# Raw token rows with a root column, and a tenth weight slot requested at the start of the expert stage

## The chip, the cores and the metric

One core of one Trainium2 chip. The metric is the device time of one launch in microseconds (us). TensorE (PE in the profile), VectorE (DVE), ScalarE (ACT), GpSimd (POOL) and SyncE (SP) run their own instruction queues and meet only at semaphores. SP's queue issues nearly all transfers between memory (HBM) and the on-chip SBUF.

## What is computed

One inference step of a two-layer decoder over 288 tokens (256 prompt tokens, 32 sample tokens), all in float32. Each layer is a mixer (gated delta rule, then differential attention) followed by a mixture of experts. The change touches only the experts, cut here to what matters:

```
xn = x * rsqrt(mean(x*x) + 1e-6) * norm_m            # per token, 1024 columns
group = argmax(softmax(xn @ w_rg + b_rg))            # 1 of 4
e1, e2 = top 2 of the 8 experts of that group; gates from a softmax
hid = silu(xn @ w_gate[e]) * (xn @ w_up[e])          # 1024 -> 512
y   = hid @ w_down[e]                                # 512 -> 1024
out = gate1 * y[e1] + gate2 * y[e2];   x = x + out
```

There are 32 experts with three matrices of 2 MB each, so each layer streams about 201 MB of expert weights.

## The kernel before

`moe_phase` runs once per layer. It walks 16 main groups of two experts, 64 token places for each expert. TensorE turns the group's 128 gathered rows (`rows_T`), multiplies them with the gate and the up matrices (`stage`, L2540), turns the hidden rows (`hid_T`), multiplies with the down matrices (`products`, L2567), and adds the result of the group before to the tokens with selection matrices (`combine`, L2583).

**Weights.** Ten slots of 2 MB in SBUF form a ring; matrix p of the stream goes to slot p mod 10, and a group uses six. Slots 0 to 8 are prefetched in the mixer phase in front (in layer 1, slots 4 and 5 at the start of the expert phase). The space of slot 9, the tenth, holds `xn`, the normalized token rows, while the phase begins. So SP stores `xn` to memory (L2078), waits for the stores and for the semaphore `gx_T` of the first picks, and only then requests slot 9 (L2083, printed as L2838, the line of the helper `prefetch`). From then on SP requests a slot when TensorE has used up its old contents: `load(10)` (L2095) in halves after the first and the second half of the first gate product, then `load_whole` (L2104) pairs of 2 MB after the first up product, the first down product, and so on. All waits and requests on SP are in order.

**Start of the phase.** TensorE transposes the tokens, makes the router logits, fills its wait with 26 products of constants (`keep_busy`, L2503), and ranks the tokens by expert (L2508 to L2513). VectorE works out the choice of experts and writes `sel0`, six 128x64 selection tiles of 0 and 1 (L2309). With these TensorE picks the first group's rows straight from `xn` in SBUF (L2626, "the first picks"), makes a table of places (L2633) and begins the first gate product. ACT meanwhile squares the rows (L2188), takes the root (L2190) and normalizes them into `xn` (L2194). POOL clears the unused rows of `xn` (L2150, L2152) and the gather buffer `xg` (L2155). `xg`, `xgT` and others lie in `xrT`, `hid` lies in `norm_row` (router inputs), and `place_o` lies in `y_sb`.

**Later groups.** POOL gathers the rows of group n from memory (L2168) after `rows_T(n-1)`; ACT applies SiLU (L2210), and VectorE multiplies it with the up product (L2382); `hid_T` waits for that.

Of the kernel before, what the change touches and what calls it, by code (L numbers as in the profile page):

```python
# [8 lines left out]
F32 = mybir.dt.float32  # L9
# [1926 lines left out]
def moe_phase(nc, m, layer):  # L1936

    ctx, sems = ExitStack(), []
    with ctx:
# [6 lines left out]
        def sem(name):  # L1946
# [9 lines left out]
        sb("late_slots", [128, SLOT_COUNT - 7, SLOT_COLS])  # L1956
        xn = sb("last_slot", [128, SLOT_COLS])[:, 0:NT * D_MODEL].rearrange("p (t d) -> p t d", t=NT)
# [51 lines left out]
        sel0 = y_sb[:, 0:NT * 128].rearrange("p (t r) -> p t r", t=NT)  # L2009
        low = y_sb[:, NT * 128:NT * 128 + SLOTS]  # L2010
        BELOW = -1024.0
        xr_flat = xrT[:].rearrange("p k r -> p (k r)")
        xg = xr_flat[:, 0:1024]
        xgT = xr_flat[:, 1024:2048].rearrange("p (k r) -> p k r", k=KT)
        obf = xr_flat[0:1, 2048:2048 + 2 * OVER_GROUPS * N_EXPERTS].rearrange("p (b e) -> p b e", e=N_EXPERTS)
        selT = w_router.rearrange("p k n -> p (k n)")[:, 0:T_ALL]
        hid = norm_b[:, 0:512]
# [23 lines left out]
            "squares ss_cleared tail_cleared roots inverse normed xn_stored xT_made xT_kept folded logits_made logits_kept gdiff gexped tdiff texped hots ranked "  # L2041
# [6 lines left out]
        def by_tile(x):  # L2048
            return x.rearrange("p (k c) -> p k c", k=KT)
# [6 lines left out]
        xn_dram = m["xn_dram"]  # L2056
# [88 lines left out]
        def _(pool):  # L2145
# [4 lines left out]
            P.memset(xn[32:64, 2, :], 0.0).then_inc(s["tail_cleared"], 1)  # L2150
            pool.wait_ge(s["tail_cleared"], 1)
            P.memset(xn[64:128, 2, :], 0.0).then_inc(s["tail_cleared"], 1)  # L2152
            pool.wait_ge(s["tail_cleared"], 2)
# [3 lines left out]
            pool.wait_ge(s["xn_stored"], 16 * NT)  # L2157
            pool.wait_ge(s["table_ready"], 1)

            def gather(n, row):  # L2160

                if not isinstance(n, int) or n > 1:
                    pool.wait_ge(s["gathered"], n * 16 - 16)
# [743 lines left out]
```

## Time and profile before

| what | value |
|---|---|
| median of 3 runs | 1517.54 us (1515.52 to 1518.78) |
| the profiled execution: time, span | 1519.84 us, 1518.0 us |
| PE busy | 1469.2 us (97%) |
| DVE, ACT, POOL busy | 634.7, 284.9, 73.0 us |
| HBM read | 483.77 MB |
| GB/s in the steady part of both expert stages | 426 to 432 |
| granted TensorE clock, mean | 0.991 |

The page divides the span into 40 slices. In slices 11 to 21 and 30 to 39 both PE and the 16 DMA engines stand at 9 of 10: these are the two expert stages. PE's busy time is modelled, so "busy" does not say by itself that PE is what limits the stage; its idle times do.

### The profile page before, as it was taken

The page shows a single profiled execution, that of the slowest core. Times are in us where ns is not written, and L with a number is a line of the kernel's source. Part 1 is how long each engine was busy: PE and PEld are TensorE (multiplying, and loading weights), DVE is VectorE, ACT ScalarE, POOL GpSimd, SP SyncE. Part 2 cuts the span into 40 slices and gives each one's busy share as a digit, 9 for nine tenths or more (in the row PEclk, how much of TensorE's full clock was granted, in tenths as well). Part 3 has the DMA queues.
Part 4 walks back from the last instruction along what each step waited for, and adds up shares of the span by engine and source line. Part 5 has one row for each costly group of instructions (what it writes and reads, how often), then busy time and mean ns, then how long its engine had stood idle before and what let it go on. Part 6 is the DMA issues. An engine that isn't in the chain of part 4 may idle for free. (4 is left out here: it accounts for less than half of the span.)

```text
span 1518.0 us, 20246 instructions
## 1 busy us (share of the span) xinstructions
PE 1469.2 (97%) x7687; PEld 735.5 (48%) x7687; DVE 634.7 (42%) x1657; ACT 284.9 (19%) x746; POOL 73.0 (5%) x123
## 2 busy tenths in 40 slices
PE   9999999999999999999999999899999999999995
PEld 7787878666333333333334445557333333333331
DVE  3666567445323324234244245735232423423324
ACT  2424243214110101001001004523010110101001
POOL 0101010001000000000000000001000000000000
PEclk9999999999999999999999999999999999999998
DMA  6432323468999999999999036695999999999993
GB/s 221 149 116 75 116 78 134 181 234 325 417 430 431 428 431 431 429 429 426 426 427 364 8 134 250 255 363 212 413 430 429 431 430 429 432 429 427 426 426 146
DMA packets 101505, 484.54 MB, mean 319 GB/s; under 512 B 16411, under 2 KB 51135, under 8 KB 67635
## 3 DMA queue, kind: packets, MB, share of 16 engines
q1 hardware_dynamic: 96818, 478.90, 77.9%
q0 software_dynamic: 4320, 4.42, 0.8%
q8 instruction: 54, 0.88, 0.2%
q14 instruction: 25, 0.20, 0.0%
q10 hardware_dynamic: 288, 0.14, 0.0%
HBM read 483.77 MB, written 10.97 MB: 326 GB/s over the span
## 5 line engine op out<-in xcount | busy, mean ns | idle before, releaser
L2540 PE MATMUL moe_ps_gate<-slots,moe_xrT 128*64 128x512 f32 x1024 | 228.1, 596 | 9.8 <-DMA slots<-in_w_gate_e_dram 9.8
L2540 PE MATMUL moe_ps_up<-slots,moe_xrT 128*64 128x512 f32 x1024 | 226.8, 595 | 0.0
L2567 PE MATMUL moe_ps_y<-slots,router_inputs 128*64 128x512 f32 x960 | 212.6, 595 | 0.0
L2413 DVE TENSOR_TENSOR resid<-resid,moe_ps_x 128x512 f32<-128x512 f32 x60 | 41.2, 687 | 254.1 <-PE moe_ps_x L2583 254.1
L2540 PEld LDWEIGHTS moe_ps_up<-slots,moe_xrT 128*64 128x64 f32 x1024 | 71.0, 137 | 151.0 <-issue 138.9
L2540 PEld LDWEIGHTS moe_ps_gate<-slots,moe_xrT 128*64 128x64 f32 x1024 | 72.4, 137 | 139.0 <-issue 137.9
L967 PE MATMUL gdn_bank<-gdn_xT,slots 128*128 128x288 f32 x512 | 136.3, 410 | 0.7 <-ACT slots L486 0.7
L2567 PEld LDWEIGHTS moe_ps_y<-slots,router_inputs 128*64 128x64 f32 x960 | 66.4, 137 | 124.8 <-issue 124.5
L2204 ACT ACTIVATE moe_xrT<-moe_ps_x,router_inputs 128x128 f32<-128x128 f32 x128 | 36.5, 367 | 379.2 <-PE moe_ps_x L2521 363.6
L967 PEld LDWEIGHTS gdn_bank<-gdn_xT,slots 128*128 128x128 f32 x512 | 92.5, 190 | 22.8 <-issue 1.1
L2382 DVE TENSOR_TENSOR router_inputs<-router_inputs,moe_ps_up 128x512 f32<-128x512 f32 x32 | 22.0, 689 | 195.0 <-PE moe_ps_up L2540 195.0
L2210 ACT ACTIVATE router_inputs<-moe_ps_gate 128x512 f32<-128x512 f32 x32 | 19.1, 597 | 222.2 <-PE moe_ps_gate L2540 222.2
L2583 PE MATMUL moe_ps_x<-moe_y_sb,router_inputs 128*128 128x512 f32 x120 | 59.5, 618 | 0.0
L2220 ACT COPY moe_y_sb<-moe_ps_y 128x512 f32<-128x512 f32 x32 | 18.7, 585 | 193.6 <-PE moe_ps_y L2567 176.6
L2405 DVE COPY moe_y_sb<-moe_ps_y 128x512 f32<-128x512 f32 x30 | 20.7, 692 | 81.3 <-PE moe_ps_y L2567 81.3
L2168 POOL DMA_INDIRECT moe_xrT<-xn_rows,moe_rows_in x30 | 30.9, 1029 | 471.0 <-PE moe_ps_x L2521 469.1
L2397 DVE TENSOR_SCALAR moe_place<-consts,moe_lpos,moe_gcur 128x128 f32<-128x128 f32 x192 | 52.1, 344 | 1.2
L2417 DVE TENSOR_TENSOR resid<-resid,moe_ps_up 32x256 f32<-32x256 f32 x112 | 46.2, 413 | 2.6
L1731 PE MATMUL at_bank<-slots,at_XK 128*128 128x512 f32 x96 | 44.0, 618 | 0.0
L1731 PE MATMUL at_pair<-slots,at_XK 128*128 128x512 f32 x96 | 41.8, 593 | 0.0
L710 DVE SCALAR_TENSOR_TENSOR slots<-slots,gdn_cw 128x312 f32<-128x312 f32 x72 | 39.2, 545 | 2.5
L2583 PEld LDWEIGHTS moe_ps_x<-moe_y_sb,router_inputs 128*128 128x128 f32 x120 | 20.3, 189 | 38.7 <-issue 38.7
(509 smaller groups left out, 1811.3 us busy)
## 6 DMA issues: line engine op xcount, KB each, us to landing
slots<-in_w_gate_e_dram SPq DMA_DIRECT2D x40, 2048.0 KB, 23.5
slots<-in_w_up_e_dram SPq DMA_DIRECT2D x40, 2048.0 KB, 23.2
slots<-in_w_down_e_dram SPq DMA_DIRECT2D x40, 2048.0 KB, 25.9
slots<-in_w_gate_e_dram SPq DMA_DIRECT2D x48, 1024.0 KB, 26.5
slots<-in_w_up_e_dram SPq DMA_DIRECT2D x48, 1024.0 KB, 26.7
slots<-in_w_down_e_dram SPq DMA_DIRECT2D x48, 1024.0 KB, 26.0
slots<-in_w_in_a_dram SPq DMA_DIRECT2D x16, 1024.0 KB, 5.5
slots<-in_w_kv_dram SPq DMA_DIRECT2D x4, 2048.0 KB, 20.1
```

What stands on the lines that cost most here:

```text
L710: ins = V.scalar_tensor_tensor(acc[:, a, j, 0:ACC_COLS], src, cw[:, a, j, tap:tap + 1], acc[:, a, j, 0:ACC_COLS], ALU.mult, ALU.add)
L967: last = T.matmul(PB[i % 2][:, 0:T_ALL], w4[:, j, k, 128 * a:128 * a + 128], xT[:, k, :], start=(k == 0), stop=(k == KT - 1))
L1731: last = T.matmul(bank[:, :], XK[:, 0 if j < 2 else 1, k, at[t]], wslot[3 * half + j][:, k, :], start=(k == 0), stop=(k == KT - 1))
L2168: pool.indirect_dma_start(xg, None, xn_dram[:, :], bass.IndirectOffsetOnAxis(rows_in[:, :], 0), bounds_check=T_ALL - 1, oob_is_err=False). ...
L2204: last = A.activation(xgT[:, k, :], ps_x[:, 1, k - 4, :], ACT.Copy, scale=norm_T[:, k:k + 1])
L2382: V.tensor_tensor(hid, hid, ps_up[:], ALU.mult).then_inc(s["hidden"], 1)
L2397: last = V.tensor_scalar(place[:, k, t, :], m["lanes"][:, :], where[:, k, t:t + 1], gcur[:, k, t:t + 1], ALU.is_equal, ALU.mult)
L2413: V.tensor_tensor(half, half, banks[i][:, :], ALU.add).then_inc(s["summed"], 1)
L2417: V.tensor_tensor(part, part, banks[i][32 * q:32 * q + 32, 0:256], ALU.add).then_inc(s["summed"], 1)
L2540: last = T.matmul(ps[64 * e:64 * e + 64, :], xgT[:, k, 64 * e:64 * e + 64], slots[:, slot[2 * n + e], 512 * k:512 * k + 512], start=(k == ...
L2567: last = T.matmul(ps_y[64 * e:64 * e + 64, h, :], hidT[:, k, 64 * e:64 * e + 64], slots[:, slot[4 + e], 1024 * k + 512 * h:1024 * k + 512 ...
L2583: last = T.matmul(banks[i][:, :], selT[:, at[t]], y_sb[:, 512 * h:512 * h + 512], start=True, stop=True)
```

## The change

Six things change in `moe_phase`, in both layers.

1. The token rows go to memory **raw** (`x_dram`, 288 rows of 1025 columns), with the inverse root of each token as column 1025, written by three more stores of 4 bytes for each row. They are staged in `norm_row`, `y_sb` and a part of `xrT` instead of in slot 9; ACT copies them without the scale, the third only after the router logits are made.
2. SP requests slot 9 as the first thing of the phase (in layer 1 right after slots 4 and 5). Before `load(10)` it waits for all six stores.
3. `sel0` holds the inverse root in place of 1: its instruction has a second per-partition operand.
4. A gathered row brings its root along. POOL copies it to `rcur` once the hidden rows of the group before are made, and from group 1 on ACT's SiLU takes it as its scale and VectorE multiplies by it (`scalar_tensor_tensor` instead of `tensor_tensor`).
5. ACT (before it keeps the first picks) and VectorE (before `overflow`) now wait for all six stores, as does POOL (before it clears `xg`). POOL's two clears of `xn` are gone, and the third tile of the first picks contracts over its 32 rows instead of 128.
6. TensorE does four more products of constants between the ranks and the first picks.

```
-        sb("late_slots", [128, SLOT_COUNT - 7, SLOT_COLS])
-        xn = sb("last_slot", [128, SLOT_COLS])[:, 0:NT * D_MODEL].rearrange("p (t d) -> p t d", t=NT)
+        sb("late_slots", [128, SLOT_COUNT - 6, SLOT_COLS])
+        low = sb("low", [128, SLOTS])
+        rcur = sb("rcur", [128, 1])
...
+        x_rows = [norm_b[:, :], y_sb[:, :], xr_flat[0:T_DEC, 0:D_MODEL]]
...
+            m["prefetch"](sp, layer, (9,))
             for t in range(NT):
-                sp.wait_ge(s["normed"], t + 1)
-                sp.dma_start(xn_dram[128 * t:128 * t + rows[t], :], xn[0:rows[t], t, :]).then_inc(s["xn_stored"], 16)
+                sp.wait_ge(s["turned_rows"], t + 1)
+                sp.dma_start(x_dram[128 * t:128 * t + rows[t], 0:D_MODEL], x_rows[t]).then_inc(s["xn_stored"], 16)
+            sp.wait_ge(s["inverse"], 1)
+            for t in range(NT):
+                sp.dma_start(x_dram[128 * t:128 * t + rows[t], D_MODEL:D_MODEL + 1], rstd[0:rows[t], t:t + 1], allow_slow_non_contiguous=True).then_inc(s["xn_stored"], 16)
             if layer == 0:
                 m["attn_inputs"](sp)
-            sp.wait_ge(s["xn_stored"], 16 * NT)
-            sp.wait_ge(s["gx_T"], 1)
-            m["prefetch"](sp, layer, (9,))
+            sp.wait_ge(s["xn_stored"], 16 * 2 * NT)
...
-            pool.wait_ge(s["logits_made"], NT)
-            P.memset(xg, 0.0).then_inc(s["cleared"], 1)
+            pool.wait_ge(s["xn_stored"], 16 * 2 * NT)
+            pool.wait_ge(s["gx_T"], 1)
+            P.memset(xg_row, 0.0).then_inc(s["cleared"], 1)
...
-                pool.indirect_dma_start(xg, None, xn_dram[:, :], bass.IndirectOffsetOnAxis(rows_in[:, :], 0),
+                pool.indirect_dma_start(xg_row, None, x_dram[:, :], bass.IndirectOffsetOnAxis(rows_in[:, :], 0),
                                         bounds_check=T_ALL - 1, oob_is_err=False).then_inc(s["gathered"], 16)
+                pool.wait_ge(s["gathered"], n * 16)
+                pool.wait_ge(s["hidden"], n)
+                pool.sem_inc(s["waits_held"], 1)
+                P.tensor_copy(rcur[:, :], xg_row[:, D_MODEL:D_MODEL + 1]).then_inc(s["r_kept"], 1)
...
-            act.wait_ge(s["inverse"], 1)
             for t in range(NT):
-                r = rows[t]
-                A.activation(by_tile(xn[0:r, t, :]), strided(resid[0:r, t, :]), ACT.Copy, scale=rstd[0:r, t:t + 1]).then_inc(s["normed"], 1)
+                if t == 2:
+                    act.wait_ge(s["logits_made"], NT)
+                A.copy(by_tile(x_rows[t]), strided(resid[0:rows[t], t, :])).then_inc(s["turned_rows"], 1)
...
+                    act.wait_ge(s["r_kept"], g)
+                    A.activation(hid, ps_gate[:], ACT.Silu, scale=rcur[:, 0:1]).then_inc(s["silued"], 1)
...
+            act.wait_ge(s["xn_stored"], 16 * 2 * NT)
             rows_kept(0)
             silu(0)
...
-                    last = V.tensor_scalar(sel0[:, t, SLOTS * e:SLOTS * e + SLOTS], low, pos0[:, t, e:e + 1], None, ALU.is_equal)
+                    last = V.tensor_scalar(sel0[:, t, SLOTS * e:SLOTS * e + SLOTS], low[:, :], pos0[:, t, e:e + 1], rstd[:, t:t + 1], ALU.is_equal, ALU.mult)
...
+                    V.scalar_tensor_tensor(hid, hid, rcur[:, 0:1], ps_up[:], ALU.mult, ALU.mult).then_inc(s["hidden"], 1)
...
+            dve.wait_ge(s["xn_stored"], 16 * 2 * NT)
             overflow()
...
+            keep_busy(4)
...
-                    last = T.matmul(ps_x[:, k // 4, k % 4, :], by_tile(xn[:, t, :])[:, k, :], sel0[:, t, :], start=(t == 0), stop=(t == NT - 1))
+                    last = T.matmul(ps_x[:, k // 4, k % 4, :], by_tile(x_rows[t])[:, k, :], sel0[0:rows[t], t, :], start=(t == 0), stop=(t == NT - 1))
```

SP's order of transfers at the start of layer 0's expert phase, before. `slots<-in_w_up_e_dram 128x2048` are the halves of slot 9, and `slots<-in_w_down_e_dram 128x2048` are those of `load(10)`:

```order
L2078 DMA xn_rows<-moe_last_slot 128x1024 x2
L2078 DMA xn_rows<-moe_last_slot 32x1024
L2852 DMA attn_inputs<-in_kv_norm_dram 128x8
L2853 DMA attn_inputs<-in_norm_b_dram 128x8
L2854 DMA attn_inputs<-in_lam_b_dram 128x256
L2855 DMA attn_inputs<-in_subln_b_dram 128x1
L2856 DMA pages<-in_page_table_dram 1x16
L2838 DMA slots<-in_w_up_e_dram 128x2048 x2
L2095 DMA slots<-in_w_down_e_dram 128x2048 x4
```

The same place of the changed kernel (L2851 is the prefetch helper, L2081 and L2084 are the stores of the rows and of the root column, L2099 is `load`):

```order
L2851 DMA slots<-in_w_up_e_dram 128x2048 x2
L2081 DMA x_rows<-router_inputs 128x1024
L2081 DMA x_rows<-moe_y_sb 128x1024
L2081 DMA x_rows<-moe_xrT 32x1024
L2084 DMA x_rows<-moe_rstd 128x1 x2
L2084 DMA x_rows<-moe_rstd 32x1
L2865 DMA attn_inputs<-in_kv_norm_dram 128x8
L2866 DMA attn_inputs<-in_norm_b_dram 128x8
L2867 DMA attn_inputs<-in_lam_b_dram 128x256
L2868 DMA attn_inputs<-in_subln_b_dram 128x1
L2869 DMA pages<-in_page_table_dram 1x16
L2099 DMA slots<-in_w_down_e_dram 128x2048 x4
```

Slot 9's two transfers have moved from behind everything to the front of the row stores, and three stores have come in.

TensorE at the same time, before, from the waiting products to the first gate product:

```order
L2503 MATMUL moe_ps_gate<-consts 128x128 x26
L2508 MATMUL moe_ps_up<-moe_both,consts 128x96
L2509 MATMUL moe_ps_up<-moe_both,consts 128x32
L2510 MATMUL moe_ps_up<-moe_both,consts 128x32
L2511 MATMUL moe_ps_up<-moe_both,consts 128x32
L2513 MATMUL moe_ps_tab<-moe_both,consts 128x32 x3
L2626 MATMUL moe_ps_x<-moe_y_sb,moe_last_slot 128x128 x24
L2633 MATMUL moe_ps_tab<-moe_entry,moe_place 128x32 x6
L2540 MATMUL moe_ps_gate<-slots,moe_xrT 64x512 x16
```

And in the changed kernel, where L2516 are the products of constants and L2639 the picks:

```order
L2516 MATMUL moe_ps_gate<-consts 128x128 x26
L2521 MATMUL moe_ps_up<-moe_both,consts 128x96
L2522 MATMUL moe_ps_up<-moe_both,consts 128x32
L2523 MATMUL moe_ps_up<-moe_both,consts 128x32
L2524 MATMUL moe_ps_up<-moe_both,consts 128x32
L2526 MATMUL moe_ps_tab<-moe_both,consts 128x32 x3
L2516 MATMUL moe_ps_gate<-consts 128x128 x4
L2639 MATMUL moe_ps_x<-moe_xrT,router_inputs 128x128
L2639 MATMUL moe_ps_x<-moe_xrT,moe_y_sb 128x128
L2639 MATMUL moe_ps_x<-moe_xrT 128x128
```

Four products stand between the counts and the picks; the picks (24 in all, of which three are shown) read three staging tiles instead of one. In the profile each of these float32 products appears as two instructions.

## Rows read from the trace of the kernel before

**Rows 1.** Waits of PE: engine, line, waited for: us in total, times, longest

```profile
PE moe_ps_gate L2540 <- DMA slots<-in_w_gate_e_dram: 9.8, 11, 1.3
```

**Rows 2.** PE in order of time, last groups of layer 0 (start, length, ..., idle before)

```profile
724.88 3.65 PE L2540 MATMUL moe_ps_gate<-slots,moe_xrT 128*64 128x512 f32 x16 [0.47 <-DMA slots<-in_w_gate_e_dram]
...
784.37 3.65 PE L2540 MATMUL moe_ps_gate<-slots,moe_xrT 128*64 128x512 f32 x16 [1.22 <-DMA slots<-in_w_gate_e_dram]
...
800.03 0.75 PE L2549 MATMUL moe_ps_hid<-consts,router_inputs 128*128 128x128 f32 x4 [0.25 <-DVE router_inputs L2382]
```

**Rows 3.** Windows: length, busy of PE, PEld, DVE, ACT, POOL, PE clock, DMA share, GB/s

```profile
362.00:366.00 4.00, 4.00 (x38) 3.96 (x36) 1.55 (x7) 1.03 (x4) 0.00 (x0) 1.00 0.05 8
366.00:368.00 2.00, 2.00 (x11) 0.82 (x12) 1.49 (x8) 1.39 (x2) 0.31 (x2) 1.00 0.93 246
382.00:388.00 6.00, 6.00 (x36) 2.69 (x36) 3.65 (x10) 1.14 (x4) 1.02 (x1) 1.00 0.99 360
420.00:700.00 280.00, 280.00 (x1296) 100.47 (x1292) 92.48 (x200) 26.67 (x70) 12.21 (x21) 1.00 1.01 430
815.00:820.00 5.00, 4.65 (x25) 3.93 (x26) 3.42 (x7) 4.44 (x7) 0.00 (x0) 0.63 1.03 379
```

**Rows 4.** SP's queue, layer 0's expert stage, in order of time

```profile
350.55 4.43 SPq L2078 DMA_DIRECT2D xn_rows<-moe_last_slot  x3
...
365.01 0.81 SPq L2838 DMA_DIRECT2D slots<-in_w_up_e_dram  x2
369.93 4.25 SPq L2095 DMA_DIRECT2D slots<-in_w_down_e_dram  x4
380.40 0.89 SPq L2104 DMA_DIRECT2D slots<-in_w_gate_e_dram  x2
```

**Rows 5.** Issue to landing: tenth slot (L2838); L2095's first, second pair; L2104's first pair

```profile
DMA to landing us min/median/max: 5.2/6.3/7.3
...
DMA to landing us min/median/max: 6.6/7.7/8.7
...
DMA to landing us min/median/max: 8.1/9.1/10.1
...
DMA to landing us min/median/max: 10.4/12.5/14.7
```

**Rows 6.** All engines in order of time, start of layer 0's expert stage

```profile
348.36 6.25 ACT L2194 ACTIVATE moe_last_slot<-resid,moe_rstd 128x1024 f32<-128x1024 f32 x3 [0.32 <-DVE moe_rstd L2264]
...
350.96 6.07 PE L2503 MATMUL moe_ps_gate<-consts 128*128 128x128 f32 x52
...
357.72 0.94 PE L2513 MATMUL moe_ps_tab<-moe_both,consts 128*128 128x32 f32 x6
...
358.12 1.07 DVE L2309 TENSOR_SCALAR moe_y_sb<-moe_y_sb,moe_pos 128x64 f32<-128x64 f32 x6
...
359.34 5.60 PE L2626 MATMUL moe_ps_x<-moe_y_sb,moe_last_slot 128*128 128x128 f32 x48 [0.67 <-DVE moe_y_sb L2309]
...
364.97 1.14 ACT L2204 ACTIVATE moe_xrT<-moe_ps_x,router_inputs 128x128 f32<-128x128 f32 x4 [7.80 <-PE moe_ps_x L2626]
...
366.23 7.09 PE L2540 MATMUL moe_ps_gate<-slots,moe_xrT 128*64 128x512 f32 x32
...
367.88 1.19 POOL L2168 DMA_INDIRECT moe_xrT<-xn_rows,moe_rows_in  x1 [0.99 <-POOL moe_rows_in L2164]
...
382.23 1.04 PE L2521 MATMUL moe_ps_x<-consts,moe_xrT 128*128 128x128 f32 x8
```

**Rows 7.** VectorE groups, shapes apart: busy us, mean ns of one

```profile
L2397 DVE TENSOR_SCALAR moe_place<-consts,moe_lpos,moe_gcur 128x128 f32<-128x128 f32 x192 | 52.1, 344 | 1.2
...
L2382 DVE TENSOR_TENSOR router_inputs<-router_inputs,moe_ps_up 128x512 f32<-128x512 f32 x32 | 22.0, 689 | 195.0 <-PE moe_ps_up L2540 195.0
...
L2317 DVE TENSOR_SCALAR moe_place<-consts,moe_lpos 128x128 f32<-128x128 f32 x12 | 2.5, 281 | 0.1
```

**Rows 8.** Issue to landing of the three row stores (L2078), layer 0

```profile
DMA to landing us min/median/max: 6.1/6.4/7.7
```

More of the change, by code:

```diff
@@ L2008, in moe_phase @@
         place_o = y_sb[:, 0:TOP_K * NT * 128].rearrange("p (k t r) -> p k t r", k=TOP_K, t=NT)
-        sel0 = y_sb[:, 0:NT * 128].rearrange("p (t r) -> p t r", t=NT)
-        low = y_sb[:, NT * 128:NT * 128 + SLOTS]
         BELOW = -1024.0
         xr_flat = xrT[:].rearrange("p k r -> p (k r)")
-        xg = xr_flat[:, 0:1024]
-        xgT = xr_flat[:, 1024:2048].rearrange("p (k r) -> p k r", k=KT)
-        obf = xr_flat[0:1, 2048:2048 + 2 * OVER_GROUPS * N_EXPERTS].rearrange("p (b e) -> p b e", e=N_EXPERTS)
+        xg_row = xr_flat[:, 0:D_MODEL + 1]
+        xg = xr_flat[:, 0:D_MODEL]
+        xgT = xr_flat[:, 1032:2056].rearrange("p (k r) -> p k r", k=KT)
+        obf = y_sb[0:1, 768:768 + 2 * OVER_GROUPS * N_EXPERTS].rearrange("p (b e) -> p b e", e=N_EXPERTS)
         selT = w_router.rearrange("p k n -> p (k n)")[:, 0:T_ALL]
+        sel0 = xr_flat[:, 1544:1544 + NT * 128].rearrange("p (t r) -> p t r", t=NT)
+        x_rows = [norm_b[:, :], y_sb[:, :], xr_flat[0:T_DEC, 0:D_MODEL]]
         hid = norm_b[:, 0:512]
@@ L2055, in moe_phase @@
         HALF = SLOT_COLS // 2
-        xn_dram = m["xn_dram"]
+        x_dram = m["x_dram"]
         W = m["expert_views"][layer]
@@ L2187, in _ @@
                 r = rows[t]
-                A.activation(xn[0:r, t, :], resid[0:r, t, :], ACT.Square, accum_out=ss[0:r, t:t + 1]).then_inc(s["squares"], 1)
+                if t == 2:
+                    act.wait_ge(s["squares"], 1)
+                A.activation(x_rows[t % 2][0:r, :], resid[0:r, t, :], ACT.Square, accum_out=ss[0:r, t:t + 1]).then_inc(s["squares"], 1)
             act.wait_ge(s["squares"], NT)
             A.activation(rstd[:, :], ss[:, :], ACT.Sqrt, scale=1.0 / D_MODEL, bias=m["eps"][:, 0:1]).then_inc(s["roots"], 1)
-            act.wait_ge(s["inverse"], 1)
             for t in range(NT):
-                r = rows[t]
-                A.activation(by_tile(xn[0:r, t, :]), strided(resid[0:r, t, :]), ACT.Copy, scale=rstd[0:r, t:t + 1]).then_inc(s["normed"], 1)
+                if t == 2:
+                    act.wait_ge(s["logits_made"], NT)
+                A.copy(by_tile(x_rows[t]), strided(resid[0:rows[t], t, :])).then_inc(s["turned_rows"], 1)
             act.wait_ge(s["gdiff"], 1)
@@ L2209, in silu @@
                 act.wait_ge(s["gate_made"], g + 1)
-                A.activation(hid, ps_gate[:], ACT.Silu).then_inc(s["silued"], 1)
+                if isinstance(g, int) and g == 0:
+                    A.activation(hid, ps_gate[:], ACT.Silu).then_inc(s["silued"], 1)
+                else:
+                    act.wait_ge(s["r_kept"], g)
+                    A.activation(hid, ps_gate[:], ACT.Silu, scale=rcur[:, 0:1]).then_inc(s["silued"], 1)
             def sel_kept(g, src):
@@ L2261, in _ @@
                     V.tensor_copy(xrT[:, 4 * j:4 * j + 4, at[t]], ps_xT[t][:, j, :, 0:rows[t]]).then_inc(s["xT_kept"], 1)
-            link(V.tensor_scalar(low, m["lanes"][:, 0:SLOTS], BELOW, None, ALU.add))
+            link(V.tensor_scalar(low[:, :], m["lanes"][:, 0:SLOTS], BELOW, None, ALU.add))
             dve.wait_ge(s["roots"], 1)
@@ L2381, in hidden @@
                 dve.wait_ge(s["silued"], g + 1)
-                V.tensor_tensor(hid, hid, ps_up[:], ALU.mult).then_inc(s["hidden"], 1)
+                if isinstance(g, int) and g == 0:
+                    V.tensor_tensor(hid, hid, ps_up[:], ALU.mult).then_inc(s["hidden"], 1)
+                else:
+                    V.scalar_tensor_tensor(hid, hid, rcur[:, 0:1], ps_up[:], ALU.mult, ALU.mult).then_inc(s["hidden"], 1)
             def turned(g):
```

14 lines of the change are left out of this document (3 added, 11 removed).

## The prediction

> **What bounds the kernel now.** The page puts PE at 97% and the DMA engines at 9 of 10 in both expert stages, so the first question is which of the two waits for the other. The waits of PE answer it: in both layers together PE stands idle 9.8 us, in 11 waits, for gate weights [rows 1]. PE in order of time shows where: layer 0 has its first such wait at 724.88 and its last at 784.37 [rows 2], all in the last groups. Until then PE never runs dry, and the windows show PE busy 280 of 280 us while the engines move 430 GB/s at a full share [rows 3]. So both are nearly even: TensorE sets the pace first, the stream of weights is a little slower, its backlog grows from group to group, and from about group 12 on the stream decides. The end of a layer is therefore the start of the unbroken weight stream, plus its bytes at 430 GB/s, plus the tail behind the last gate weights. Work of PE in front of group 12 only eats into its later waits; what delays the start of the stream, or what lies in the tail, counts in full.
>
> The second question is where the unbroken stream starts. The windows show the engines idle from 362 to 366 (share 0.05), since SP asks for the tenth slot only at 365.01 [rows 3, 4]. That looks like 2 MB, or 4.9 us at 430 GB/s, to be won in each layer. SP's own queue says otherwise. The next request, the first pair of L2095, goes out at 369.93, because it waits for TensorE to use up half of slots 0 and 1, and TensorE begins its gate product at 366.23 [rows 4, 6]. The tenth slot has landed by 365.4 + 7.3 = 372.7, and the four halves behind it by about 373.8 + 10.1 = 383.8 [rows 5]. The request after those, at 380.40, waits for TensorE's up product. Its first 2 MB land 10.4 us later, at 390.8 [rows 4, 5], which is 7.0 us behind 383.8 where 2.1 MB at 430 GB/s take 4.9. From 382 to 388 the engines move only 360 GB/s [rows 3]. I read this as a backlog that has just run out when L2104's first pair arrives: **the stream that decides the end begins with the request at 380.40**, which PE's progress sets, and not with the tenth slot.
>
> **The change, part by part.**
>
> *Tenth slot first.* The 4.9 us go into idle time of the engines in front of 366, but PE's requests behind it go out when they did. What can be won is what the tenth slot holds up today. Its two halves land 7.7 us after the first was asked for (365.01 to 372.7) from idle engines. The first pair behind it needs 369.93 to about 370.4 + 8.7 = 379.1, or 9.2 us [rows 4, 5]. With idle engines it too would need 7.7, so 1.5 us at most would be passed on, if the backlog at 380.40 is real; nothing, if it has run out. I take 0, nearer to the drop to 360 GB/s, and keep 0 to 1.5 us of gain for each layer.
>
> *The second operand of `sel0`.* On 128 columns a `tensor_scalar` takes 281 ns with one per-partition operand and 344 ns with two [rows 7], 63 ns more. Six stand one behind the other in front of the first picks (358.12 to 359.19), and the picks wait for the last of them, 0.67 us idle [rows 6]. Six times 0.06 is 0.36 us. All behind it follow: picks, table, first gate product, and with it every weight request. **+0.36 us in each layer**; bounds 0.2 (part of it overlaps) and 0.5.
>
> *Four products of constants.* 52 instructions take 6.07 us [rows 6], so eight take 0.93. The counts end at 358.66, so they end at 359.59; `sel0` is ready at 359.55 and the picks would begin at 359.70. Cost 0, hidden by the longer `sel0`. If `sel0` costs nothing more, they themselves delay the picks by 0.25; this is in the bounds above.
>
> *Stores and the new waits.* ACT's copies start at about 348.1 rather than 348.36, since they need no reciprocal, and end near 354.4; the same 6.25 us [rows 6]. The stores now stand behind slot 9. The slowest landed 7.7 us after its request [rows 8]; the last row store was issued near 354.6 and landed about 361. With 4.9 us of weights in front it lands near 366. The three root stores are issued about a microsecond later and land, if they behave like the row stores, at 366 to 367. Who waits: ACT, whose part of the first picks takes 1.14 us and is needed by the second half of the gate product, at 366.23 + 0.36 + 3.55 = 370.1, so the stores may come as late as 369.0; SP, which has nothing to ask for before 370.3; VectorE, whose `overflow` has over 7 us until its result is used at 380; POOL, which clears `xg` for about 1 us and gathers at about 369 instead of 367.88. That gather is needed by `rows_T(1)` at 382.23 [rows 6]; even with the 10.1 us of the slowest half that lands in the full stream [rows 5] it is there at 379. Cost 0, with 2 us of room on ACT in layer 0. In layer 1 the last weight request in front of slot 9 is older by some microseconds, so there is more room.
>
> *The root in every group.* The multiply by `rcur` adds one operand to L2382: 689 ns and, by the same 63 ns, about 0.75 us [rows 7]. `hid_T` waits for it. In groups 1 to 14 that is 14 times 0.06, or 0.8 us for each layer, and PE's waits for weights [rows 1] take it up. In the last group nothing does: PE waits 0.25 us for this very instruction at 800.03 [rows 2]. **+0.06 us in each layer.** SiLU's scale lies a whole up product in front of its reader. POOL's copy of the root fits between the hidden rows and the next gather, which waits for `rows_T` anyway.
>
> *Longer gathered rows.* 4100 instead of 4096 bytes are 0.1% of a gather. Rows that start at odd places might go slower: in the steady stream 36 rows of 4 KB (576 picks in 16 groups) are 0.34 us at 430 GB/s. Taken as 0, with that much again for each of 15 gathers, 5 us a layer, as the far bound.
>
> The sum: (0.36 + 0.06) x 2 = **+0.8 us**. On the profiled execution's 1519.84 us this gives 1520.7; the median of the runs shown is 1517.54, 2.3 us lower, and against it the time is **1518.4 us**.
>
> **A rule that speaks against the change.** No store of 4 bytes to memory stands in the rows, and the row stores are full lines. The Trainium skill (DMA: Bandwidth & Descriptors, the table of key figures) says that transfers need 512 bytes or more for full rate, and that the engines read, modify and write below that. No run here shows it yet. By that rule the 288 root writes are slow, but the sum would be changed only if they took more than the 2 us of room; that is the second rival below.
>
> **The rivals.**
>
> *The stream really starts with the tenth slot* (faster). Then each layer wins what PE waits for weights, 9.8 us in both [rows 1], and the time is 1517.5 + 0.8 - 9.8 = 1508.5. The full share from 366 on speaks for it [rows 3]; PE's requests at 369.93 and 380.40 speak against it. A partial gain of 1.5 us a layer gives 1515.4, inside my forecast. Chance of the full or a large gain: 0.09.
>
> *The stores come late* (slower). If the root stores add as much again as the slowest row store, 7.7 us [rows 8], behind slot 9's end near 363.5, they land at 371.2. ACT then keeps its half of the picks at 372.3, the gate product stops 2.2 us at its middle, and the first pair of L2095 is late by as much. This decides from a landing after 369.0; beyond it each microsecond costs one. A granted clock that falls after such a stop would cost more: between 815 and 820 the clock is 0.63 after an idle stretch of PE [rows 3], and at half the rate 3.4 us of work take 6.8. Time 1518.4 + 2.2 = 1520.6 in layer 0 alone, up to 1524 with the 3.4 us of a fallen clock. Chance 0.12.
>
> *Gathers of odd rows are slow*: up to 5 us a layer, 1520 to 1528. The gathers' share of the traffic is small. Chance 0.04.
>
> *The change does not take effect as said*: the tenth slot stays behind something else, since SP's queue is in order. It costs or gives nothing beyond the 0.8, and lies in the forecast.
>
> **How the numbers follow.** A measurement of this kernel can tell about 0.2%, or 3.0 us, from no change; the runs before spread over 3.3 us. Forecast (0 to 1.5 us of gain a layer, +0.8): 0.75, nearly all within 3.0 us. Faster by more than 0.2%: 0.09 from the first rival and 0.03 from the spread of runs. Slower: 0.12 half beyond the line, 0.03 of 0.04 from the gathers, and 0.06 from the spread and from bounds that add up. That is 0.12 faster, 0.73 same, 0.15 slower. The range takes in the forecast with the partial gain and the spread of runs, 1514.0, and the late stores in one layer, 1522.5.
>
> **What would show it right or wrong.** Right: the engines idle between the tenth slot's end and about 371; PE's waits for gate weights are still 8 to 10 us; the first request of L2104's counterpart comes about 0.4 us later against the start of the phase; the hidden multiply takes about 0.75 us. Wrong: PE's waits for weights go down by 4 us or more (first rival), or PE stops at the middle of the first gate product, or ACT stands idle for the stores beyond 369 (second).

## The result, and the profile after

| | before | changed |
|---|---|---|
| median of 4 runs each | 1517.24 us (1515.52 to 1518.78) | 1529.11 us (1525.10 to 1531.69) |
| ratio, 95% interval | | 1.0076 [1.0059, 1.0093] |
| profiled execution: time, span | 1519.84, 1518.0 us | 1525.10, 1522.9 us |
| granted TensorE clock, mean | 0.991 | 0.994 |
| PE busy | 1469.2 us | 1476.4 us |

The change costs 11.9 us between the medians. 1518.4 was forecast, 0.8 us slower than before, with a range up to 1522.5: the direction came out as forecast, the size did not. A loss of more than 0.2% had a chance of 0.15; it is 0.76%.

PE is busy 7.2 us longer while the granted clock of the profiled execution is higher, so some work on PE itself has become longer. PE in order of time, with VectorE's `sel0` and ACT's part of the picks, at the start of layer 0's expert stage of the changed kernel (it answers to [rows 6]; here the phase begins 1.8 us later than there):

```profile
359.88 1.43 DVE L2318 TENSOR_SCALAR moe_xrT<-moe_low,moe_pos,moe_rstd 128x64 f32<-128x64 f32 x6
360.36 1.16 PE L2516 MATMUL moe_ps_gate<-consts 128*128 128x128 f32 x8
361.46 0.46 PE L2639 MATMUL moe_ps_x<-moe_xrT,router_inputs 128*128 128x128 f32 x2
361.76 0.39 PE L2639 MATMUL moe_ps_x<-moe_xrT,moe_y_sb 128*128 128x128 f32 x2
362.07 0.48 PE L2639 MATMUL moe_ps_x<-moe_xrT 32*128 32x128 f32 x2
362.49 0.49 PE L2639 MATMUL moe_ps_x<-moe_xrT,router_inputs 128*128 128x128 f32 x2
362.81 0.39 PE L2639 MATMUL moe_ps_x<-moe_xrT,moe_y_sb 128*128 128x128 f32 x2
363.13 0.48 PE L2639 MATMUL moe_ps_x<-moe_xrT 32*128 32x128 f32 x2
...
369.46 0.48 PE L2639 MATMUL moe_ps_x<-moe_xrT 32*128 32x128 f32 x2
369.87 1.64 PE L2646 MATMUL moe_ps_tab<-moe_entry,moe_place 128*128 128x32 f32 x12
370.04 1.14 ACT L2208 ACTIVATE moe_xrT<-moe_ps_x,router_inputs 128x128 f32<-128x128 f32 x4 [11.11 <-PE moe_ps_x L2639]
370.10 0.95 POOL L2156 MEMSET moe_xrT<- 128x1025 f32 x1 [24.59 <-PE moe_ps_x L2639]
371.44 7.09 PE L2554 MATMUL moe_ps_gate<-slots,moe_xrT 128*64 128x512 f32 x32
373.10 1.20 POOL L2166 DMA_INDIRECT moe_xrT<-x_rows,moe_rows_in  x1 [1.01 <-POOL moe_rows_in L2162]
```

`sel0` takes 1.43 us instead of 1.07, and the four idle products lie in the gap as planned. The picks then take from 361.46 to 369.94 (where the last row, 369.46 and 0.48 long, ends), 8.48 us, where they took 5.60. They were the same 24 products by number. The row of before was one row of 48 instructions; now the view splits at every change of tile or shape, and the starts can be read: three products from 361.46, the next three from 362.49, on average 8.48 / 8 = 1.06 us for three. Before it was 5.60 / 8 = 0.70. The same instructions as the trace groups them by form, with shortest/median/longest in ns (each float32 product is two of them), first of the changed kernel:

```profile
L2639 PEld LDWEIGHTS moe_ps_x<-moe_xrT,router_inputs x16: 186/188/189, 361.4 to 368.9; 128*128 128x128 f32 x16
L2639 PE MATMUL moe_ps_x<-moe_xrT,router_inputs x16: 275/312/377, 361.5 to 369.0; 128*128 128x128 f32 x16
L2639 PEld LDWEIGHTS moe_ps_x<-moe_xrT x16: 181/182/184, 362.1 to 369.6; 32*128 32x128 f32 x16
L2639 PE MATMUL moe_ps_x<-moe_xrT x16: 270/321/372, 362.1 to 369.7; 32*128 32x128 f32 x16
```

and before:

```profile
L2626 PEld LDWEIGHTS moe_ps_x<-moe_y_sb,moe_last_slot x48: 186/192/192, 359.3 to 364.5; 128*128 128x128 f32 x48
L2626 PE MATMUL moe_ps_x<-moe_y_sb,moe_last_slot x48: 275/275/348, 359.3 to 364.7; 128*128 128x128 f32 x48
```

The third tile now contracts over 32 rows (item 5 of the change). Its weight load and its shortest product are no slower than those of 128 rows; what grows is the step from one product to the next. Taken one by one, the instructions from the second product on start at 361.76, 361.87, 362.07 (32 rows), 362.29 (32 rows), 362.49, 362.70 and 362.81. Between equal row counts a step is 0.11 us; the step into another row count is 0.20, and the one behind it 0.21. The weight loads show the same place: between equal row counts the load begins 0.11 us before its product, while the product before still runs; at a change the load (362.071) and its product (362.072) begin together.

The first gate product stands 26.59 us behind the phase's first transposes in layer 0 and 26.62 in layer 1, where it stood 23.15 and 23.18: 3.44 us in each layer. 0.36 of it is `sel0`, some 2.9 the picks, and 0.1 the table products, which now follow on a product of 32 rows.

SP's queue at the start of layer 0's expert stage (it answers to [rows 4]):

```profile
344.80 0.81 SPq L2851 DMA_DIRECT2D slots<-in_w_up_e_dram  x2
351.77 0.33 SPq L2081 DMA_DIRECT2D x_rows<-router_inputs  x1
...
356.06 1.36 SPq L2084 DMA_DIRECT2D x_rows<-moe_rstd  x3
...
375.18 4.27 SPq L2099 DMA_DIRECT2D slots<-in_w_down_e_dram  x4
```

The windows in the gap, with the columns of [rows 3]:

```profile
367.00:370.00 3.00, 3.00 (x19) 2.27 (x19) 0.00 (x0) 0.00 (x0) 0.00 (x0) 1.00 0.07 17
370.00:375.00 5.00, 5.00 (x30) 2.64 (x32) 3.08 (x15) 2.43 (x5) 2.37 (x3) 1.00 0.00 0
375.00:378.00 3.00, 3.00 (x18) 1.00 (x16) 2.83 (x18) 0.00 (x0) 0.00 (x0) 1.00 0.70 182
```

The tenth slot is asked for at 344.80 instead of 365.01, and the engines are idle from about 367 until PE, at 375.18, lets SP ask for more. The landings of the three root stores:

```profile
DMA to landing us min/median/max: 11.1/11.2/12.2
```

The last of them is issued at 357.0, so the stores have landed by 369.2 at the latest, while ACT's first use of the picks comes at 370.04 and waits for PE. The waits of PE for gate weights, which were 9.8 us in 11 waits [rows 1]:

```profile
PE moe_ps_gate L2554 <- DMA slots<-in_w_gate_e_dram: 8.2, 9, 1.4
```

And PE in order of time in the last group of layer 0, where 0.25 stood [rows 2]:

```profile
806.07 0.75 PE L2563 MATMUL moe_ps_hid<-consts,router_inputs 128*128 128x128 f32 x4 [0.31 <-DVE router_inputs L2394]
```

### The profile page after: what moved, and what is told of

Same layout as the page of the kernel before. It is cut to its first block and busy times, and to the rows that moved or that the text cites. A ratio compares the mean times of both kernels' runs of the same rounds, so it can differ in the third digit from the quotient of the medians.

```text
span 1522.9 us, 20374 instructions
## 1 busy us (share of the span) xinstructions
PE 1476.4 (97%) x7703; PEld 738.3 (48%) x7703; DVE 637.8 (42%) x1657; ACT 287.2 (19%) x746; POOL 74.9 (5%) x149
## 5 line engine op out<-in xcount | busy, mean ns | idle before, releaser
L2394 DVE SCALAR_TENSOR_TENSOR router_inputs<-router_inputs,moe_rcur,moe_ps_up 128x512 f32<-128x512 f32 x30 | 22.4, 747 | 183.4 <-PE moe_ps_up L2554 183.4
L2218 ACT ACTIVATE router_inputs<-moe_ps_gate,moe_rcur 128x512 f32<-128x512 f32 x30 | 20.6, 687 | 208.5 <-PE moe_ps_gate L2554 208.5
L2171 POOL COPY moe_rcur<-moe_xrT 128x1 f32<-128x1 f32 x30 | 5.5, 183 | 687.1 <-DVE router_inputs L2394 662.8
```

Of the source, the lines that this page charges most:

```text
L2394: V.scalar_tensor_tensor(hid, hid, rcur[:, 0:1], ps_up[:], ALU.mult, ALU.mult).then_inc(s["hidden"], 1)
```

## The experiments

**Theory:** each change of the row count inside the picks costs PE some 2.9 us a layer, and the rest follows from PE being late. **Rivals:** the early tenth slot or the stores disturb something; the idle products cost; the gathers or the hidden multiply do. "Gate product" is the distance from the phase's first transposes to the first gate product, layer 0/1, in the profiled execution; "stages" the length of the two expert stages from the first transposes on (in layer 0 to the first product of the next mixer, in layer 1 to the last product of the experts).

| kernel | median us | ratio to before | gate product | stages |
|---|---|---|---|---|
| before | | | 23.15/23.18 | 472.27/471.14 |
| changed | 1529.11 | 1.0076 [1.0059, 1.0093] | 26.59/26.62 | 476.52/473.66 |
| changed, again | 1527.98 | 1.0071 [1.0054, 1.0088] | 26.58/26.57 | 475.94/473.63 |
| changed, third tile whole | 1517.90 | 0.9997 [0.9986, 1.0008] | 23.51/23.51 | 472.76/470.18 |
| before, third tile of 32 rows | 1538.58 | 1.0120 [1.0087, 1.0152] | 32.27/33.36 | 482.86/483.62 |
| changed, 32-row products in pairs | 1521.47 | 1.0015 [1.0001, 1.0028] | 25.05/25.07 | 474.99/472.29 |
| whole tile, no idle products | 1519.89 | 1.0006 [0.9993, 1.0019] | 23.54/23.51 | 472.48/470.84 |
| changed, no idle products | 1542.52 | 1.0148 [1.0122, 1.0173] | 33.14/33.16 | 485.00/483.89 |
| changed, six idle products | 1527.64 | 1.0076 [1.0062, 1.0090] | 26.85/26.88 | 477.24/475.65 |
| whole tile, tenth slot late | 1517.57 | 1.0007 [0.9998, 1.0016] | 23.49/23.49 | 472.80/471.18 |

### The third tile whole again

```
-            V.memset(ss[:], 1.0).then_inc(s["ss_cleared"], 1)
+            V.memset(ss[:], 1e36).then_inc(s["ss_cleared"], 1)
...
-                    last = T.matmul(ps_x[:, k // 4, k % 4, :], by_tile(x_rows[t])[:, k, :], sel0[0:rows[t], t, :], start=(t == 0), stop=(t == NT - 1))
+                    last = T.matmul(ps_x[:, k // 4, k % 4, :], by_tile((x_rows[0], x_rows[1], xg)[t])[:, k, :], sel0[:, t, :], start=(t == 0), stop=(t == NT - 1))
```

The third tile contracts over 128 rows again; its 96 unused rows get an inverse root of about 3e-17 (the square root of 1e36 / 1024, turned over), so what lies in them weighs nothing. All else of the change stays.

> The changed kernel, but the third tile of the first picks contracts over all 128 rows of the staging buffer (rows 32 to 127 of its selection tile are made negligible by a huge mean square there). Theory 1, a product over 32 rows between products over 128 rows holds up TensorE: the 48 picks take 5.6 us again instead of 8.5, the gate product starts 2.9 us earlier in each layer, and the time falls by about 6 us or more, to within 3 us of the kernel before. Theory 2, the loss lies elsewhere (late stores, gathers, the extra operand, the clock): picks may get faster, but the time stays at about 1529 us.

1517.90 us against 1518.57 for the kernel before. PE in the same place:

```profile
357.77 1.16 PE L2516 MATMUL moe_ps_gate<-consts 128*128 128x128 f32 x8
358.87 0.46 PE L2639 MATMUL moe_ps_x<-moe_xrT,router_inputs 128*128 128x128 f32 x2
359.17 0.39 PE L2639 MATMUL moe_ps_x<-moe_xrT,moe_y_sb 128*128 128x128 f32 x2
359.39 0.39 PE L2639 MATMUL moe_ps_x<-moe_xrT 128*128 128x128 f32 x2
359.61 0.39 PE L2639 MATMUL moe_ps_x<-moe_xrT,router_inputs 128*128 128x128 f32 x2
```

Steps of 0.22 us, picks of 5.60 us, and the gate product 0.36 and 0.33 us later than before instead of 3.44. So the row count alone made the kernel slower; all the rest of the change together costs nothing that can be measured. ACT in this kernel shows that the stores are not far from mattering:

```profile
366.46 1.14 ACT L2208 ACTIVATE moe_xrT<-moe_ps_x,router_inputs 128x128 f32<-128x128 f32 x4 [10.12 <-DMA x_rows<-moe_rstd]
```

The picks end at 364.47, and ACT begins 2.0 us later, for it waits for the root stores. It is done at 367.60, and the gate product, which begins at 365.77, needs that at its middle, at about 369.3: 1.7 us of room.

### The row count alone, in the kernel before

```
-                    last = T.matmul(ps_x[:, k // 4, k % 4, :], by_tile(xn[:, t, :])[:, k, :], sel0[:, t, :], start=(t == 0), stop=(t == NT - 1))
+                    last = T.matmul(ps_x[:, k // 4, k % 4, :], by_tile(xn[0:rows[t], t, :])[:, k, :], sel0[0:rows[t], t, :], start=(t == 0), stop=(t == NT - 1))
```

> The kernel before, with one edit: the third tile of the first picks contracts over its 32 rows. Theory 1: picks take 8.5 us instead of 5.6, the gate product starts 2.9 us later in each layer, and the time rises by 6 us or more, to 1523 to 1529 us. Theory 2: no change, 1517 us.

1538.58 us against 1518.57 for the kernel before in the same batch: 20.0 us slower, nearly twice the price of the whole change, and 10 us beyond the 1523 to 1529 expected. PE, and a window of the same stretch (columns as in [rows 3]):

```profile
359.53 13.25 PE L2626 MATMUL moe_ps_x<-moe_y_sb,moe_last_slot 128*128 128x128 f32 x48 [0.68 <-DVE moe_y_sb L2309]
372.71 2.90 PE L2633 MATMUL moe_ps_tab<-moe_entry,moe_place 128*128 128x32 f32 x12
375.54 8.71 PE L2540 MATMUL moe_ps_gate<-slots,moe_xrT 128*64 128x512 f32 x32
```

```profile
362.00:366.00 4.00, 4.00 (x15) 3.10 (x14) 1.65 (x9) 0.00 (x0) 0.00 (x0) 0.50 0.00 0
366.00:370.00 4.00, 4.00 (x15) 2.99 (x13) 0.08 (x1) 0.00 (x0) 0.00 (x0) 0.50 0.00 0
```

The picks take 13.25 us, not 8.5, because the granted clock is 0.50, the lower of its two levels (1.2 GHz), from 361.8 on for 17.1 us, and in layer 1 from 1058.1 for 20.5 us. Up to 361.8, at full clock, three products take 1.055 us, as in the changed kernel. PE counts as busy all the while. What it did before the fall: 0.68 us idle and then the slow picks. The kernel before has a gap of 0.67 us there too, and fast picks, and its clock stays at 1.00 [rows 3]. The same edit therefore has two prices: its own 2.9 us a layer, and a fall of the clock that it lets in.

### The 32-row products in pairs

```
-                for t in range(NT):
+                tiles = (0, 1, 2) if k % 2 == 0 else (2, 1, 0)
+                for t in tiles:
```

`start` and `stop` go by the first and the last of `tiles`. This halves the changes of row count, from 16 to 8, with the same products.

> The changed kernel with the order of the three tiles turned round in every second step, so that the 32-row products of two steps stand next to each other: the same 24 picks, half as many changes between 32 and 128 rows. If the change of rows costs, picks take about 7.1 us (half of the 2.9 us is gone) and the time falls by about 3 us. If a 32-row product is slow by itself, picks stay at 8.5 us and the time stays.

1521.47 us, 1.0015 of before. The pieces of the picks:

```profile
358.71 0.46 PE L2640 MATMUL moe_ps_x<-moe_xrT,router_inputs 128*128 128x128 f32 x2
359.00 0.39 PE L2640 MATMUL moe_ps_x<-moe_xrT,moe_y_sb 128*128 128x128 f32 x2
359.32 0.71 PE L2640 MATMUL moe_ps_x<-moe_xrT 32*128 32x128 f32 x4
359.96 0.49 PE L2640 MATMUL moe_ps_x<-moe_xrT,moe_y_sb 128*128 128x128 f32 x2
360.28 0.61 PE L2640 MATMUL moe_ps_x<-moe_xrT,router_inputs 128*128 128x128 f32 x4
```

The gate product comes at 25.05, 1.54 us earlier than in the changed kernel: half of what the picks and the table had lost. So the cost goes by changes of row count: 16 of them (the last is the one to the table) cost 3.1 us, 8 of them 1.5, about 0.19 us each. 32 rows by themselves are not slow. The time falls by 7.6 us, where 3 were expected; the picks account for 3.1 of it in the two layers, and the rest is the second price, the clock, for which the section on the changed kernel run again has the numbers.

### The idle products

```
-            keep_busy(4)
```

Taken out of the version with the whole tile and of the changed kernel.

> The first experiment's kernel without the four products of constants. By the sum of the prediction they are covered by the longer selection: picks start at the same time and the time equals the first experiment's. If the clock needs them, some runs show half clock behind the gap of about 1 us and are 2 to 4 us longer.

> The changed kernel without its four products of constants, 32-row picks kept. If the gap of about 1 us in front of the slow picks is what lets the clock fall, as it did in the second experiment, picks take 12 us or more at half clock in both layers, and the time is 1536 to 1542 us. If the four products do nothing, it stays at 1529 us.

With the whole tile it is 1519.89 us, 1.0006 [0.9993, 1.0019]: no difference from the kernel before that can be told, though PE now has a gap of 1.03 us. Against the 1517.90 with the four products it is 2.0 us more, with a mean granted clock of 0.9927 instead of 0.9937; its profile has full clock at the picks, so whether the clock falls there in other executions stays open. In the changed kernel it is 1542.52, 13.4 us more than with them (14.5 against the 1527.98 of its second set). PE there:

```profile
359.91 0.46 PE L2638 MATMUL moe_ps_x<-moe_xrT,router_inputs 128*128 128x128 f32 x2 [1.03 <-DVE moe_xrT L2318]
...
361.65 0.79 PE L2638 MATMUL moe_ps_x<-moe_xrT 32*128 32x128 f32 x2
362.38 0.80 PE L2638 MATMUL moe_ps_x<-moe_xrT,router_inputs 128*128 128x128 f32 x2
```

And the window behind it:

```profile
362.00:366.00 4.00, 4.00 (x14) 3.00 (x13) 1.43 (x10) 0.00 (x0) 0.00 (x0) 0.50 0.75 248
```

The steps double from 361.65 on: the clock falls at 361.4 for 20.5 us, and again in layer 1, at 1064.6, for as long. So the four products, at which I set down a cost of 0, are what keeps the slow picks from costing twice as much. In these profiles the gap and the slow picks together bring the fall, and the gap with fast picks does not. The profile with six idle products, below, has one fall behind slow picks without any gap.

### The changed kernel again, and with six idle products

> The changed kernel itself once more, for its spread. By the theory of two parts, the slow picks cost about 3.4 us in each layer in every run, and in some runs the clock also falls behind them, each fall costing 6 to 9 us: runs spread from 1522 to 1540 us, in steps, wider than those of the kernel before; median 1525 to 1532. Against it: if the rest over the 7 us comes from something steady, all runs lie within 3 us of 1529.

1527.98 us with six runs from 1525.03 to 1531.78; its profile shows 26.58/26.57 and no fall at the picks, as the first did. The spread is narrower than the 1522 to 1540 expected, and steps of 6 to 9 us cannot be seen in it. The two profiled executions are the fastest of their sets. Their expert stages are 6.8 and 6.2 us longer than before's, while the medians differ by 11 to 12 us. The rest has to be in the other executions. The profiled times differ by only 5.3 us; before's profile is a long execution of its kernel, with half clock for 27.8 us in all against 19.5 in the changed kernel's, in both outside the expert stages.

```
-            keep_busy(4)
+            keep_busy(6)
```

> The changed kernel with six idle products in front of the first picks instead of four. Two more take 0.23 us (two of four instructions-pairs at 0.117 us each), in each layer, on the path: +0.5 us. Open is what the difference between the changed kernel's profile (1525.0 us) and its median (1528 to 1529 us) is. Theory A (in some runs the clock still falls at the slow picks, since four idle products are only just enough): two more products make the falls rare, the runs close up at 1525.5 to 1526.5, the mean granted clock of nearly all is 0.993 or more, median 1526. Theory B (the spread has nothing to do with the picks; it is the falls elsewhere that the kernel before also shows): the runs spread as before, 1525.5 to 1532, median 1528.5 to 1529.5, with mean clocks down to 0.988 again.

1527.64 us, with runs up to 1530.50 and mean clocks down to 0.989: two more products do not help, as theory B said. But its profile caught what theory A spoke of, in layer 1. PE behind the last picks, and the window:

```profile
1058.52 1.64 PE L2646 MATMUL moe_ps_tab<-moe_entry,moe_place 128*128 128x32 f32 x12
1060.09 8.78 PE L2554 MATMUL moe_ps_gate<-slots,moe_xrT 128*64 128x512 f32 x32
```

```profile
1060.00:1065.00 5.00, 5.00 (x18) 1.65 (x19) 4.26 (x22) 1.14 (x1) 1.30 (x2) 0.66 0.14 35
```

The first gate product takes 8.78 instead of 7.09 us, since the clock is at half for 3.4 us right behind the picks. PE had no gap before those picks. The runs' mean clocks tell how much this makes over many executions. Half clock costs (1 - mean clock) x span, if PE's work sets the time there. The mean of the runs' times less that is 1508.3 us for 23 runs of the kernel before and 1515.1 us for the 10 runs of the changed one (the runs of the kernel before beside the other experiments give 1509.1 to 1509.6). That is 5.5 to 6.8 us of longer work, as in the profiles. What is left is clock: 0.9942 on average before and 0.9913 now, 0.0029 x 1528, or 4.4 us, known to about 2. The two make 10 to 11 us, and the medians differ by 10.8 to 11.9.

The same sum for the other kernels, in us lost to half clock in a mean run, beside the kernel before in the same set:

| kernel | lost | kernel before |
|---|---|---|
| changed, 10 runs | 13.3 | 8.8 |
| changed, six idle products | 12.5 | 7.7 |
| changed, 32-row products in pairs | 9.3 | 9.6 |
| changed, third tile whole | 9.6 | 9.6 |
| whole tile, no idle products | 11.1 | 9.6 |
| before, third tile of 32 rows | 23.8 | 9.6 |
| changed, no idle products | 26.5 | 8.4 |

So the second price is tied to the row counts as the first is, and with half of the changes it is gone: that is why the pairs gained more than twice what was expected. Against theory B, the changed kernel loses more to the clock than the kernel before does. Where in the single executions the clock fell is shown only by the one profile above; for the others it is inferred.

### What the tenth slot is worth

```
-            m["prefetch"](sp, layer, (9,))
             for t in range(NT):
...
             sp.wait_ge(s["xn_stored"], 16 * 2 * NT)
+            sp.wait_ge(s["gx_T"], 1)
+            m["prefetch"](sp, layer, (9,))
```

From the version with the whole tile.

> The first experiment's kernel, with the tenth slot requested again where it was before, behind the stores and the first picks. By the prediction the early request is worth 0 to 1.5 us in each layer, taken as 0: time equal to the first experiment within 1 us, at most 3 us more. If the unbroken stream really started with the tenth slot, this kernel would be 9 us slower than the first experiment.

1517.57 us against 1517.90 with the early request, each 1.00 of before. Expert stage of layer 0: 472.80 against 472.76; of layer 1: 471.18 against 470.18. Worth 0.0 and at most 1.0 us, inside the 0 to 1.5 a layer of the prediction.

### Trials at a faster version

If the stream starts with the request at 380.40, that request can be made earlier. Matrices 12 and 13 are then asked for in halves too, `load(12)` before the pairs, without and with the whole tile of the changed kernel:

```
-        WHOLE = (12, 72)
+        WHOLE = (14, 74)
...
             load(SLOT_COUNT)
+            load(12)
...
```

(What is left out are TensorE's waits for the second halves.)

> The kernel before, with the weight request behind the first up product (matrices 12 and 13 of the stream) sent as two halves, the first of them already after half of the up product. By the prediction the stream runs dry just before this request and the unbroken stream starts with it: the first half would be asked for 3.5 us earlier, the 2.1 us that the landings lack would be filled, and the waits for gate weights fall by 1 to 2 us in each layer; time 2 to 4 us below the kernel before. If there was a real backlog at that point, nothing changes.

> The first experiment's kernel with the same two halves. If the stream no longer runs dry behind the first up product, the early tenth slot can pass its 1.5 us on: 3 to 7 us below the first experiment. If the early slot is worth nothing in any case, it gains what the third kernel of this group gains.

1515.35 us, 0.9991 [0.9982, 1.0000], for the kernel before with halves, whose expert stages are 0.67 and 0.66 us shorter; 1517.42, 0.9998 [0.9988, 1.0007], with both. The first is 2.1 us below the kernel before in its set, where 2 to 4 were expected, the second 0.5 below the first experiment, where 3 to 7 were. The place may be right, but the gain is at the edge of what can be told: PE's waits for gate weights went from 9.8 to 8.7 us, and with the whole tile from 7.4 to 5.9. Little was gained either by moving the table products (L2633) out of the way, into the first gate product, where the gate product then begins 1.4 us earlier:

> The kernel before with the two halves of the third experiment of the last group, and the table of places (12 instructions, 1.5 us) moved from in front of the first gate product to its middle. The gate product, and with it every weight request, starts 1.3 us earlier; the gather that needs the table has over 5 us of room. Expected 1 to 1.3 us less in each layer than with the halves alone, 1511 to 1514 us.

> The changed kernel with whole third tile, halves, and the table in the middle of the first gate product. Risk: the wait for the six stores now lies closer, since the gate product's second half needs ACT's part of the picks by about 368.4 in the time of the profile before, and the stores land near 366 to 368. If they are in time, 1511 to 1515 us; if not, ACT and PE stand idle for them and the gain of the table is gone.

1516.60 us, 0.9995 [0.9984, 1.0006], and 1517.04, 0.9995 [0.9984, 1.0005], both above what was expected. The stages were 471.51/469.92 and 471.70/470.21 us: 0.1 and 0.6 us shorter than with the halves alone in the kernel before, 0.2 and 0.3 longer with the whole tile. Why the 1.4 us were not passed on stays open. The picks with the 32-row products behind each other in each half of the picks, with three changes of row count in them instead of fifteen, have no time: in that order new sums are opened in a PSUM bank (PSUM is the memory that TensorE adds up in) where others are still open, and these would lose their partial sums. That the cost falls further with fewer changes than eight is thus not shown. No version beats the kernel before by more than the 0.2% that can be told.

## Why the prediction was wrong

**The step that failed** is item 5 of the change, "the third tile of the first picks contracts over its 32 rows". The part-by-part reckoning has no term for it: it lets the picks follow `sel0` at their old 5.60 us. They take 8.48. None of the rivals holds it either, so the range could not. No product of the picks before had 32 rows, and by its count of 24 products the order of the two kernels is alike. But its shapes are not, and a changed operand shape in a series that stands on the path should have been bounded like any unseen operation: from 0 to, say, one product's own time for each change, 16 x 0.275 = 4.4 us a layer. That would have made the range reach 1527, still 2 us short of the median, and given the slower side a mechanism.

A better bound stood in the trace of the kernel before, in the table products right behind the picks. Four of the six contract over 128 rows and the last two over 32:

```profile
364.77 0.98 PE L2633 MATMUL moe_ps_tab<-moe_entry,moe_place 128*128 128x32 f32 x8
365.68 0.63 PE L2633 MATMUL moe_ps_tab<-moe_entry,moe_place 32*128 32x32 f32 x4
```

The last of the eight starts at 365.47, 0.11 behind its neighbour; the first with 32 rows comes 0.21 behind it, the next 0.13, the others 0.11 again, and the gate product, with 128 rows, 0.20 behind the last. An estimate from these steps is 0.1 us for each change, or 1.6 us a layer for 16. That is about half of what came (these products have 32 columns, the picks 128; whether this makes the difference is not shown), but it is not 0, and it is a term for the sum.

The prediction weighed a rule that speaks against the change, but not the one that bears on this step. The Trainium skill (TensorEngine Tiling (Array Packing), Key Properties) says that changing the tiling mode, and not only the tile, drains TensorE. The runs agree as to the price, if a contraction over 32 rows counts as another mode: about 0.19 us for each change of row count, nothing for 32 rows that follow on 32 rows. The Trainium skill (TensorE: Matmul & The Clock Gate, LDWEIGHTS) says that loading 32x128 weights takes as long as 128x128. That too agrees, 182 ns against 188, but it is the price of one instruction and not of the series.

**A second omission** is that the clock can fall without an idle stretch. The prediction named a fallen clock as a supplement to late stores, from [rows 3]. Here it follows slow picks, in one profile with no idle time of PE before them, and makes some 4 of the 11 us.

Point by point:

- *PE's progress sets the start of the stream.* Held. PE was 3.44 us later at the gate product, SP's first pair with it, and the stages are 4.3 us (layer 0) and 2.5 us (layer 1) longer, though PE had 9.8 us of waits for weights. Of 6.9 us of delay in front of the stream, 6.8 came out at the end. The sign named for it, L2104's counterpart 0.4 us later against the start of the phase, came out at 3.4 (40.75 instead of 37.32).
- *Tenth slot worth 0, up to 1.5 us a layer.* Held: 0.0 and 1.0. The engines stand idle from 370 to 375.
- *`sel0` +0.36 us.* 1.43 less 1.07 is 0.36, and the whole-tile version's gate product is 0.36 and 0.33 us later.
- *Idle products cost 0.* Held for their own cost (gate product 23.51 with and 23.54 without, on the whole tile); that they would be worth 13 to 14 us to the slow picks was not seen.
- *Stores land at 366 to 367, needed by 369.0.* Nearly right. The last root store landed at 369.2 in the changed kernel, whose phase begins 1.8 us later, and at 366.4 in the version with the whole tile, whose phase begins 0.8 us earlier: 367.3 to 367.4 by the clock of the profile before. The three took 11.1 to 12.2 us, and landed up to 2.2 us behind the last row store. With the whole tile ACT waits for them until 366.46 and has 1.7 us of room left, near the 2 of the prediction, and nothing is lost. In layer 1 there is hardly more room: the last landed 24.0 us behind the first transposes, and 24.4 in layer 0. The rival of late stores is a real mechanism that stayed under its point of decision.
- *Multiply by the root 0.75 us.* 747 ns. In the last group PE waits 0.31 us instead of 0.25, the 0.06 of the sum.
- *Gathers of 4100 bytes cost 0.* Held, within what the whole-tile version (0.9997) can tell.
- *PE's waits for gate weights still 8 to 10 us.* 8.2, and 7.7 in the second profile. This sign was right and said nothing of the loss, which lies ahead of them.

Without the failed step the sum can be tested: it gave +0.8 us, a ratio of 1.0005; the version with the whole tile has 0.9997 [0.9986, 1.0008].

## What to carry to other kernels

When a change alters the shape of an operand in a series of products, price the series, not the product: the steps between neighbours are where the time is. Look in the trace at hand for any place where the two shapes already meet, and read the step there. Fewer rows in a contraction save nothing here, and alternating row counts cost; pad to one row count with weights that are next to nothing, as in the version with the whole tile, or put products of one shape together. Where a slower series stands behind a gap on TensorE, look at the granted clock of several executions, since the fall that follows can cost more than the series itself.

## What was not expected of the hardware

- A change between contractions of 128 and of 32 rows costs TensorE about 0.19 us at full clock with 128 columns (16 changes 3.1 us, 8 changes 1.5 us): the step into the change is 0.20 us and the one behind it 0.21, instead of 0.11, and at the change the weight load no longer begins ahead of its product.
- The granted clock went to half for 17.1 and 20.5 us, with PE busy, behind 0.68 or 1.03 us idle and the slow picks; in the profiles it did not behind the same gaps with fast picks. Four small products in the gap (1.16 us) kept it at 1.00 in both profiles of the changed kernel; with six, and no gap, it fell for 3.4 us in one layer.
- Stores of 4 bytes for each row, behind 2 MB of weights, took 11.1 to 12.2 us to land, about as long as the row stores ahead of them (11.3 to 14.3).
